# Routed experts in a transformer block on one Trainium2 core: one block of rows per turn of the loop, single buffers, no rounding up

## What is computed

```python
    expert = g_sel * EXPERTS_PER_GROUP + e_sel          # two of 32 experts for each of T = 2048 tokens
    flat_e = expert.reshape(-1)
    counts = jnp.bincount(flat_e, length=N_EXPERTS)
    padded = (counts + EXPERT_BLOCK - 1) // EXPERT_BLOCK * EXPERT_BLOCK      # EXPERT_BLOCK = 128
    ...
    def expert_block(inp):
        xb, e = inp                                      # 128 rows of 1024, one expert
        hmid = jax.nn.silu(xb @ w_gate[e]) * (xb @ w_up[e])      # 1024 x 512 each
        return hmid @ w_down[e]                          # 512 x 1024
    ...
    y = yb.reshape(-1, D)[row] * gate.reshape(-1)[order][:, None].astype(x.dtype)
    return jnp.zeros((T, D), x.dtype).at[tok].add(y).reshape(B, L, D)
```

```
111 82 99 116 118 121 127 122 125 129 135 147 149 117 127 121
139 171 149 137 147 134 139 168 113 95 127 113 116 137 130 135
```

## Time and profile before

| | us |
|---|---|
| median of 3 executions | 2950.09 (2949.94 to 2951.58) |
| the profiled execution, its time | 2950.91 |
| the profiled execution, its span | 2948.7 |
| TensorE busy in the span | 2637.4 (89%) |
| DVE busy | 1801.0 (61%) |
| ACT busy | 1278.0 (43%) |
| POOL busy | 945.9 (32%) |
| first gate product of the experts' stage | 1750.41 |
| last product of the experts' stage ends | 2720.08 |

### The profile page before, as it was taken

How to read it: one execution, slowest core, us unless ns; L and a number is a source line. 1 busy time by engine, 2 the same in 40 slices (tenths; PEclk the granted TensorE clock), 3 DMA queues, 4 the chain that set the end, 5 groups by cost and what they waited for, 6 DMA issues and landing times. The chain is left out here.

```text
span 2948.7 us, 34628 instructions
## 1 busy us (share of the span) xinstructions
PE 2637.4 (89%) x10976; PEld 1662.6 (56%) x10977; DVE 1801.0 (61%) x2352; ACT 1278.0 (43%) x2298; POOL 945.9 (32%) x929
## 2 busy tenths in 40 slices
PE   6988879999967878778799869999999999998998
PEld 3634323346833444444588736666666666665787
DVE  2186999699965766776322287664554444741676
ACT  2377858959845555665322232222222222221322
POOL 1477968500010111111000015444444434531321
PEclk9999989999977989999699979999999999999999
DMA  5102121112152022212544376986586665972664
GB/s 149 60 27 55 26 54 33 51 52 70 61 165 75 27 66 78 83 65 67 181 143 143 117 279 249 354 331 220 215 318 228 220 220 203 344 297 80 200 215 135
DMA packets 221792, 439.11 MB, mean 149 GB/s; under 512 B 22952, under 2 KB 91112, under 8 KB 221544
## 3 DMA queue, kind: packets, MB, share of 16 engines
q1 hardware_dynamic: 199432, 357.78, 35.4%
q0 software_dynamic: 13456, 47.85, 5.2%
q10 hardware_dynamic: 8784, 31.99, 2.7%
HBM read 331.67 MB, written 105.91 MB: 148 GB/s over the span
## 5 line engine op out<-in xcount | busy, mean ns | idle before, releaser
L2395 DVE CAST p_high<-p_low 128x2048 fp32r<-128x2048 f32 x128 | 203.1, 1587 | 393.4 <-PE p_psG L2489 293.6
L688 PE MATMUL p_psP<-home,p_ring 128*128 128x512 f32 x832 | 366.1, 598 | 0.0
L2505 PE MATMUL p_psY<-p_wd,p_hT 128*128 x768 | 337.9, 593 | 2.1 <-ACT p_hT L2565 1.9
L2397 DVE TENSOR_TENSOR p_low<-p_low,p_high 128x2048 fp32r<-128x2048 f32 x128 | 319.9, 2499 | 4.4
L688 PEld LDWEIGHTS p_psP<-home,p_ring 128*128 128x128 f32 x832 | 157.2, 191 | 205.0 <-issue 204.8
L2505 PEld LDWEIGHTS p_psY<-p_wd,p_hT 128*128 128x128 f32 x768 | 142.2, 190 | 163.7 <-issue 163.5
L2428 POOL TENSOR_TENSOR p_hid<-p_act_g,p_act_u 128x512 f32<-128x512 f32 x48 | 62.5, 1302 | 529.1 <-ACT p_act_u L2560 276.8
L717 PE MATMUL p_psI<-p_kI,p_qI 64*128 64x512 f32 (+3 forms) x608 | 150.9, 605 | 63.4 <-ACT p_relu L579 63.3
L2422 POOL TENSOR_TENSOR p_xT_low<-p_xT,p_xT_high 128x512 fp32r<-128x512 f32 x96 | 189.6, 1993 | 3.6 <-ACT p_xT L2550 3.6
L2487 PE MATMUL p_psG<-p_high,p_xT_high 128*128 128x512 f32 x384 | 171.2, 446 | 17.0 <-DVE p_low L2397 9.3
L786 DVE TENSOR_SCALAR_CACHE_REDUCE p_equal<-p_S_low,p_flip 128x512 uint8<-128x512 f32 (+4 forms) x139 | 168.7, 1213 | 0.0
(11 more groups left out here) (414 smaller groups left out, 5643.0 us busy)
## 6 DMA issues: line engine op xcount, KB each, us to landing
p_low<-in_w_expert_gate_dram SPq DMA_DIRECT2D x32, 2048.0 KB, 13.4
p_low<-in_w_expert_up_dram SPq DMA_DIRECT2D x32, 2048.0 KB, 17.0
p_wd<-in_w_expert_down_dram SPq DMA_DIRECT2D x32, 2048.0 KB, 10.8
y_dram<-p_y ACTq DMA_DIRECT2D x48, 512.0 KB, 8.1
p_xt<-in_x_dram SPq DMA_DIRECT2D x32, 512.0 KB, 4.7
y_dram<-p_clear SPq DMA_DIRECT2D x32, 512.0 KB, 4.6
proj_f<-p_stage SPq DMA_DIRECT2D x52, 256.0 KB, 2.4
p_ot<-o_dram SPq DMA_DIRECT2D x16, 512.0 KB, 4.2
```

The lines of the kernel that those rows point to most:

```text
L688: mm = pe.matmul(psP[0:n, i % 2, :], w, aT[:, k, c * CH:(c + 1) * CH], start=k == 0, stop=k == KD - 1)
L2395: dve.tensor_copy(high[:, m, k, :], low[:, par, m, k, :].bitcast(F32)).then_inc(high_done, 1)
L2397: dve.tensor_tensor(low[:, par, m, k, :], low[:, par, m, k, :].bitcast(F32), high[:, m, k, :].bitcast(F32), ALU.subtract).then_inc(w_split, 1)
L2505: mm = pe.matmul(psY[:, c, :], hT[:, par, k, :], wd[:, bass.ds(at, 1), k, c * CH:(c + 1) * CH].rearrange("p a f -> p (a f)"), start=k == 0 ...
```

## The change

The loops of TensorE, ACT and POOL do one block per turn. The number of turns is the number of blocks less two, without rounding up, so the two lines that corrected the tables go. `hid`, `hT`, `y` and `slot` have one buffer, and so have their semaphores; of `xb` the second half holds block 1 alone, and all later gathers go to the first half. What a buffer's next writer waits for is one block later accordingly. The core of the diff:

```diff
             after(dve.tensor_reduce(be[:, 0:NBX], cmpb[:, :, :], AX, ALU.add))
-            after(tsc(odd[:, 1:2], order[:, NE - 1:NE], -1.0, None, ALU.add))
-            after(tsc(be[:, 0:NBX], be[:, 0:NBX], odd[:, 1:2], None, ALU.min))
-            after(stt(out=cmp16[:, 0:2, :].rearrange("p a j -> p (a j)"), in0=iota[:, 0:NBLK // 2], scalar=2.0,
-                      in1=nbi[:, NE - 1:NE].broadcast_to([P, NBLK // 2]), op0=ALU.mult, op1=ALU.is_lt))
-            after(dve.tensor_reduce(be[:, NBX:NBX + 1], cmp16[:, 0:2, :].rearrange("p a j -> p (a j)"), AX, ALU.add))
-            after(stt(out=odd[:, 0:1], in0=be[:, NBX:NBX + 1], scalar=2.0, in1=nbi[:, NE - 1:NE], op0=ALU.mult, op1=ALU.subtract))
-            after(tsc(be[:, NBX:NBX + 1], be[:, NBX:NBX + 1], -1.0, None, ALU.add))
+            after(tsc(last[:, :], order[:, NE - 1:NE], -1.0, None, ALU.add))
+            after(tsc(be[:, 0:NBX], be[:, 0:NBX], last[:, :], None, ALU.min))
+            after(tsc(be[:, NBX:NBX + 1], nbi[:, NE - 1:NE], -2.0, None, ALU.add))
...
-            after(tsc(cmpb[:, 0:1, :].rearrange("p a e -> p (a e)"), full[:, :], nbi[:, NE - 1:NE], odd[:, 0:1], ALU.is_equal, ALU.mult))
-            after(tt(full[:, :], full[:, :], cmpb[:, 0:1, :].rearrange("p a e -> p (a e)"), ALU.add))
...
-            def gather(b, par, it, turns, carried):
-                pool.wait_ge(slot_set[par], it)
-                pool.wait_ge(turned, turns)
-                pool.wait_ge(carrier_set, carried)
+            def gather(b):
+
+                pool.wait_ge(slot_set, b - 1)
+                pool.wait_ge(turned, b * 2)
+                pool.wait_ge(carrier_set, b + 1)
...
-                pool.wait_ge(hT_turned, b)
-                pool.tensor_tensor(hid[:, par, :], act_g[:, :], act_u[:, :], ALU.mult).then_inc(h_done, 1)
+                pool.wait_ge(hT_turned, b + 1)
+                pool.tensor_tensor(hid[:, :], act_g[:, :], act_u[:, :], ALU.mult).then_inc(h_done, 1)
...
-            with pool.Fori(0, m) as it:
-                for par in range(2):
-                    b = it * 2 + par
-                    gather(b + 2, par, it + 1, b * 2 + 2, b + 3)
-                    pool.wait_ge(x_loaded[1 - par], (it + par) * 16 + 16)
-                    load_slots(b + 3, 1 - par)
-                    hidden(b + 1, 1 - par)
-                    split_x(b + 2)
-            hidden(m * 2 + 1, 1)
+            with pool.Fori(0, m) as b:
+                gather(b + 2)
+                pool.wait_ge(x_loaded[0], b * 16 + 32)
+                load_slots(b + 3)
+                hidden(b + 1)
+                split_x(b + 2)
+            hidden(m + 1)
...
-            with pe.Fori(0, m) as it:
-                for par in range(2):
-                    b = it * 2 + par
-                    e, at = expert(b + 1)
-                    product(b + 1, GATE, e, at)
-                    turn_h(b, par)
-                    product(b + 1, UP, e, at)
-                    turn_x(b + 2, par, it + 1)
-                    e, at = expert(b)
-                    down(b, par, e, at)
+            with pe.Fori(0, m) as b:
+                e, at = expert(b + 1)
+                product(b + 1, GATE, e, at)
+                turn_h(b)
+                product(b + 1, UP, e, at)
+                turn_x(b + 2, 0, b * 16 + 32)
+                e, at = expert(b)
+                down(b, e, at)
...
-                act.wait_ge(y_done, b * 2 + 2)
-                act.activation(hT[:, par, :, :], psH[:, :].rearrange("p (k t) -> p k t", t=P), ACT.Copy).then_inc(hT_done, 1)
+                act.wait_ge(y_done, b * 2 + 4)
+                act.activation(hT[:, :, :], psH[:, :].rearrange("p (k t) -> p k t", t=P), ACT.Copy).then_inc(hT_done, 1)
...
-            def output(b, par, it):
-                act.wait_ge(y_stored[par], it * 16 + 16)
+            def output(b):
+                act.wait_ge(y_stored, b * 16 + 16)
```

More of the change, by code:

```diff
@@ L2023, in route @@
         full, order = sb("full", [P, NE]), sb("order", [P, NE])
-        odd = sb("odd", [P, 2])
+        last = sb("last", [P, 1])
         pos = sb("pos", [P, NT, NE])
@@ L2324, in experts @@
         slots, xb, x_loaded = gathers
-        slot = sb("slot", [P, 2], I32)
+        slot = sb("slot", [P, 1], I32)
         xT = sb("xT", [P, KD, P])
@@ L2337, in experts @@
         psY = ctx.enter_context(nc.psum_tensor("p7_psY", [P, 2, CH], F32))
-        slot_set = [sem(f"slot_set{b}") for b in range(2)]
+        slot_set = sem("slot_set")
         wg_split = sem("wg_split")
@@ L2347, in experts @@
         y_copied = [sem(f"y_copied{c}") for c in range(2)]
-        y_stored = [sem(f"y_stored{b}") for b in range(2)]
+        y_stored = sem("y_stored")
         block = ctx.enter_context(nc.Block())
         def rounds(eng):
-            return eng.value_load(blocks[0:1, NBX:NBX + 1], min_val=1, max_val=NBLK // 2 - 1)
+            return eng.value_load(blocks[0:1, NBX:NBX + 1], min_val=1, max_val=NBLK - 2)
         @block.sync
@@ L2495, in turn_h, with down @@
                 for k in range(KF):
-                    mm = pe.transpose(psH[:, k * P:(k + 1) * P], hid[:, par, k * P:(k + 1) * P], ident[:, :])
+                    mm = pe.transpose(psH[:, k * P:(k + 1) * P], hid[:, k * P:(k + 1) * P], ident[:, :])
                 mm.then_inc(hT_turned, 1)
-            def down(b, par, e, at):
+            def down(b, e, at):
                 pe.wait_ge(hT_done, b + 2)
@@ L2512, in _ @@
             product(0, UP, e, at)
[L2513 removed]
+            turn_x(1, 1, 16)
             m = rounds(pe)
[L2515 to L2534 removed]
+            with pe.Fori(0, m) as b:
[6 more added lines that the diff above has]
+                down(b, e, at)
+            e, at = expert(m + 1)
+            product(m + 1, GATE, e, at)
+            turn_h(m)
+            product(m + 1, UP, e, at)
+            e, at = expert(m)
+            down(m, e, at)
+            turn_h(m + 1)
+            e, at = expert(m + 1)
+            down(m + 1, e, at)
         @block.scalar
         def _(act):
[L2538 to L2539 removed]
+            act.sem_inc(y_stored, 16)
             def copy_x(b):
@@ L2580, in _ @@
             m = rounds(act)
-            with act.Fori(0, m) as it:
-                for par in range(2):
-                    b = it * 2 + par
-                    silu(b + 1)
-                    copy_h(b, par)
-                    copy_u(b + 1)
-                    copy_x(b + 2)
-                    output(b, par, it)
-            b = m * 2
-            silu(b + 1)
-            copy_h(b, 0)
-            copy_u(b + 1)
-            output(b, 0, m)
-            copy_h(b + 1, 1)
-            output(b + 1, 1, m)
+            with act.Fori(0, m) as b:
+                silu(b + 1)
+                copy_h(b)
+                copy_u(b + 1)
+                copy_x(b + 2)
+                output(b)
+            silu(m + 1)
+            copy_h(m)
+            copy_u(m + 1)
+            output(m)
+            copy_h(m + 1)
+            output(m + 1)
 def finish_weights(nc, outer, ctx):
```

61 lines of the change are left out of this document (23 added, 38 removed).

## The result

| | before | after |
|---|---|---|
| median, side by side | 2950.09 us (5 executions, 2942.13 to 2951.58) | 2924.51 us (5, 2917.91 to 2932.48) |
| ratio, 95% interval | | 0.9918 (0.9899 to 0.9937) |
| profiled execution, its time | 2950.91 us | 2930.01 us |
| its span | 2948.7 us | 2928.3 us |
| mean of all executions timed in this study | 2948.1 us (75, standard deviation 3.9) | 2924.5 us (17, 4.3) |

The kernel is faster by 25.6 us in the medians that stand side by side, and by 2948.1 - 2924.5 = 23.6 us (give or take 2.2) in the means of all executions. The forecast was 20.56 us and 2929.5 us; the time lies 5.0 us under the forecast and 2.0 us under the range.

The account below looks back on a forecast made before the run. TensorE sets the pace at 19.37 us a block, weight arrival at 21.20 us where experts have one block. Padding block 19.36 + DVE chain 1.20 = 20.56 us, others 0: 2950.09 - 20.56 = 2929.5 us, range 2926.5 to 2934.

Parts of the forecast that it names:

- the padding block: Experts' stage, last expert: 47 blocks run instead of 48, so what follows moves up by 19.36 us.
- the chain on DVE: End of the routing, before the experts can start: fewer small DVE steps, 1.20 us saved, bounds 0 and 1.2.
- y, whose stores the prediction read for a wait: ACT's copy of a block's result now waits for the previous block's store, slowest landing 13.6 us: 0 us.
- xb, hid, hT, slot: Other buffers cut to one: waits already met, or on Pool covered with 1.0 us left in the tightest case: 0 us.
- 22 more turns: Branches back on four engines, 45 turns instead of 23: 0 us, at most 2.06 us a time.
- base: Median of the runs before, 2950.09 us, from which the 20.56 us were subtracted.
- Rival B: Loop's branch back with register reload: each added turn costs up to 2.06 us, 2974.8 us in all; chance 0.04.
- Rival C: Experts' loop: no block saved since the count is even, only the DVE chain gains, 2948.9 us; chance 0.02.
- Rival A: Pool's closed single-buffer chain gets late and TensorE waits: 3 to 10 us given back, middle 2935 us; chance 0.09.
- the new wait: Pool, before overwriting the single slot, waits for the gather it has just issued: 0 us, as Pool is otherwise idle.
- 1 or 2 us for where TensorE's clock rises: Allowance, shared with the barriers, in the forecast's own width of 2927 to 2933 us.
- The span of the profiled execution: Whole kernel's profile: 2948.7 - 20.6 = 2928.1 us; more than 6 us away would make the sum wrong.

Follow-up runs that it names:

- e2_padding: The kernel after with one turn more, so that the padding block 48 is run again; median 2944.14 us, ratio 0.9987 to the kernel before.
- e3_chain: The kernel after with ten more steps (12.6 us) at the end of DVE's routing chain; mean 2935.7 us, ratio 0.9959 to the kernel before.
- e7_pool6: The kernel after with six more 128 x 512 multiplications on Pool per turn, before the multiplication into hid; median 3130.9 us, ratio 1.0621 to the kernel before.
- e5_const: The kernel before, two blocks per turn, with only the kernel after's shorter DVE chain; mean 2947.0 us, ratio 0.9993 to the kernel before.
- e11_again: The kernel after, unchanged, timed again in a further comparison; median 2924.03 us, ratio 0.9916 to the kernel before.

## Why the prediction was wrong in its number and right in its reasons

| step of the prediction | forecast | shown |
|---|---|---|
| the padding block | 19.36 us | 19.36 in the trace (42 to last), 19.5 by e2_padding |
| the chain on DVE | 1.20 us, all carried | 1.20 in the traces; e3_chain carries 10.9 of 12.6 (give or take 4) |
| y, whose stores the prediction read for a wait | 0 | no wait, but the first store quicker: a gain of about 1.0 (loop or buffer, not separated) |
| xb, hid, hT, slot | 0 | 0; no wait of TensorE for Pool |
| 22 more turns | 0 | 0; 19.37 us per block with one turn each |
| base | 2950.09 us | 2948.1, mean of 75 |

**The mechanism held.** One block less and a shorter chain are 20.56 of the 23.6 us. Rival B (turns cost) fell: it would have made every period longer, and they are 19.37 us. The prediction read 160 us without a packet of instructions; from 1820 to 2640 us, 41 blocks, the traces before and after have four such packets each, so none is fetched with each turn. Rival C fell with the 47 multiplications. Rival A did not occur, though the new wait is there, 220 us of it on Pool, and e7_pool6 shows what it would have looked like. The rule that stood beside A, to double-buffer for performance (the Trainium skill, Trainium Kernel Development and Optimization, best practices), is not borne out here: going to one buffer cost nothing in any trace, and where it made Pool wait, Pool had nothing else to do.

**What failed is the size of two terms: the base, and the 0 us for y.** Of the 5.0 us by which the time lies under the forecast, 2.0 are the base: I took the median of three executions as if it were known to 0.2 us, since the three lay close together. About 1.0 is the first store: the prediction read its landing of 13.6 us and asked only whether the next copy into y would have to wait for it, and put down 0. It did not ask why one store of 48 took 13.6 us when the typical one took 8.1, nor why its issue took 5.86 us, nor whether the new loop would issue it at another moment. (Whether the request moved by the loop of one block or by y's single buffer is not separated; e5_const, with the shorter chain alone, has the slow store.) The remaining 2.0 us, 23.6 - 19.36 - 1.20 - 1.0, lie within the uncertainty of the means (2.2), and their cause is open. From block 0 to block 42 the two profiles of the kernel before take 844.3 and 844.2 us, the three of the kernel after and e2_padding 841.4 to 842.6, on average 2.4 less. Of this 1.15 is the step from block 2 to 3, where the first store shows, 0.8 the step before it, where the clock rises and which e11_again has as long as before, and 0.5 is spread over the rest. The first product of block 0 starts at 1750.4 and 1748.6 us before, and at 1749.7, 1746.7 and 1745.7 us after, a scatter as large as what is sought.

**The range was too narrow.** It was 2926.5 to 2934.0, its near end set by "1 or 2 us for where TensorE's clock rises". A median of five executions with a standard deviation of 4.3 us is itself uncertain by several us, and a base of three executions by more. The three executions of before didn't show that spread. The prediction allowed for the clock only where it rises in this stage; but over the whole kernel the longer executions have the lower mean granted clock, and the stage's first product starts up to 10 us earlier or later (last section).

**One agreement was chance.** The span of the profiled execution was forecast at 2928.1 us and was 2928.3. It contains the 1.7 us of the last down product at the lower clock and a block 0 that started later than in the other two profiles (1749.67 against 1746.73 and 1745.74 us); those have spans of 2922.4 and 2923.2 us.

## What to carry to other kernels

A padded unit of work that the loop's shape adds costs a whole period of the engine that sets the pace, and removing it was worth just that here, read off as the distance of two starts; the buffers given up for it cost nothing if the writer already stands behind the reader in its engine's order, and the next thing to ask is how much work the now closed chain could still take. Ask of an outlier in the trace (one store of 48 that takes 13.6 us) not only whether it does harm but what makes it one, since a change nearby may remove it. And take a base of three executions as uncertain by the spread of the kernel, not by theirs.

## What the runs showed of the hardware

The instruction that issues a DMA can itself be held for microseconds. The first store of the stage on ACT's queue, 1.14 to 1.15 us after a load on SP's, was held for 5.4 to 5.9 us and landed after 12.8 to 13.6 us; 0.84 to 0.85 us after, it was held for 0.40 us and landed after 8.3 to 8.7 us in the kernel after. With added copies of ACT in front (1.38 and 1.57 us) it was 5.2 and 4.6 us, landing after 12.3 and 12.5. Later stores with such lags were issued in 0.34 to 0.35 us.
A multiplication of 128 x 512 on Pool takes 1.1 us alone and 2.5 us while DVE casts and subtracts 128 x 2048, whose subtraction in turn goes from 2.29 to 3.01 us.
Executions of one program, on one core each of several chips, differ by a standard deviation of 3.9 us in 2948 (75 executions). In the profiles whose code ahead of the stage is that of the kernel after, the first product of the experts' stage starts between 1742.3 and 1752.3 us, so much of this spread arises ahead of the stage. It goes with TensorE's clock: the fastest four of the kernel after's 17 executions have a mean of 2918.9 us and a granted clock of 0.9557, the slowest four 2930.6 us and 0.9515. What sets the clock in one execution and not in another was not tried.
